# The 96 slots of an expert block laid on 128 partitions, three of each four, with ranks dealt round sixteen groups of partitions

## What is computed

```
xn2 = rmsnorm(x, ffn_norm_w)                    # (1088, 1024)
grp = argmax(xn2 @ w_rg + b_rg)                 # one of 4 groups
top_v, top_i = top_k(expert logits of that group (8), 2)
w   = softmax(top_v) * p_grp
expert_id = grp * 8 + top_i                     # 2 of 32 experts a token
for each block of tokens of one expert e:
    xb = xn2[idx]
    yb = (silu(xb @ w_gate[e]) * (xb @ w_up[e])) @ w_down[e]
y = x + sum over a token's two choices of w * yb
```

## Time and profile before

| | |
|---|---|
| time before, median of 3 runs | 1531.64 us (1528.09 to 1534.46) |
| the profiled execution, its own time | 1530.42 us |
| its span | 1528.7 us |
| mean granted TensorE clock | 0.977 |
| busy, share of the span: PE, DVE, ACT, POOL | 94%, 67%, 46%, 30% |
| weight queue (q1): moved, share of 16 DMA engines | 322.10 MB, 62.1% |
| row queue (q0): moved, share | 29.21 MB, 6.2% |

### The profile page before, as it was taken

One profiled execution on the slowest core, in us unless ns is written; L12 is line 12 of the kernel. 1 busy time (PEld: TensorE's weight loads), 2 busy tenths in 40 slices (PEclk: granted clock), 3 DMA queues, 4 the chain that ended last, 5 costly groups with the idle time before them and its releaser, 6 DMA issues.

```text
span 1528.7 us, 21704 instructions
## 1 busy us (share of the span) xinstructions
PE 1431.5 (94%) x8070; PEld 1207.7 (79%) x8070; DVE 1019.8 (67%) x1387; ACT 702.0 (46%) x830; POOL 458.9 (30%) x372
## 2 busy tenths in 40 slices
PE   7999999999999999999999789989999999999993
PEld 6899999989999998898887667767766666666662
DVE  4422321166677777777566889979988788888882
ACT  6321121154445544323121266757666666666670
POOL 1600000021111112001100475466755454555543
PEclk9999999999999999999999799999999999999996
DMA  5345449244333325676733799999999999999971
GB/s 195 117 154 167 160 160 104 97 148 137 106 101 101 101 76 149 186 241 212 314 119 124 249 355 375 382 362 365 363 357 353 348 351 346 349 360 354 369 276 32
DMA packets 156588, 352.34 MB, mean 230 GB/s; under 512 B 32098, under 2 KB 110374, under 8 KB 130849
## 3 DMA queue, kind: packets, MB, share of 16 engines
q1 hardware_dynamic: 134744, 322.10, 62.1%
q0 software_dynamic: 21248, 29.21, 6.2%
q10 hardware_dynamic: 536, 0.26, 0.1%
HBM read 308.80 MB, written 87.17 MB: 259 GB/s over the span
## 4 chain that ended last, share of the span: by engine, by line
DMA 24%; PE 19%; issue 4%; POOL 3%; DVE 2%; ACT 0%; POOLq 0%; ACTq 0%; SPq 0%; DVEq 0%
DMA w_out<-in_w_down_e 15%; DMA w_gate<-in_w_gate_e 2%; PE xt_ey L2794 1%; DVE e_w_lo L2648 1%; PE xt_ey L2796 1%; PE xt_ey L2795 1%; DMA y_rows<-group_rows,slot_table 1%; DMA first_rows<-y_rows 1%; POOL slot_info L2497 1%; DMA y_prompt<-y_rows,slot_table 1%; PE y_x L2202 1%; PE y_h_up L2202 1%; PE y_x L2204 1%; PE y_h_up L2204 1%; PE y_x L2203 1%
## 5 line engine op out<-in xcount | busy, mean ns | idle before, releaser
L2648 DVE TENSOR_TENSOR e_w_lo<-mixed,e_w_hi 128x2048 fp32r<-128x2048 f32 x64 | 145.2, 2286 | 11.5 <-ACT e_w_hi L2593 11.2
L2593 ACT CAST e_w_hi<-w_out 128x2048 fp32r<-128x2048 f32 x64 | 122.2, 1910 | 53.1 <-DMA w_out<-in_w_down_e 50.4
L2648 DVE TENSOR_TENSOR e_w_lo<-w_out,e_w_hi 128x2048 fp32r<-128x2048 f32 x64 | 143.8, 2284 | 2.2 <-ACT e_w_hi L2593 2.2
L2593 ACT CAST e_w_hi<-mixed 128x2048 fp32r<-128x2048 f32 x62 | 117.3, 1910 | 44.6 <-DMA mixed<-in_w_gate_e 30.9
L1018 PE MATMUL gate_banks<-f_hi,wg_hi 128*128 128x364 f32 (+1 forms) x376 | 126.8, 337 | 0.9 <-PEq L186 0.5
L2794 PE MATMUL xt_ey<-e_w_hi,e_hT_hi 128*96 128x512 f32 x256 | 105.0, 410 | 22.1 <-DVE e_w_lo L2648 22.1
L1019 PE MATMUL gate_banks<-f_lo,wg_hi 128*128 128x364 f32 (+1 forms) x376 | 123.5, 328 | 0.0
L1020 PE MATMUL gate_banks<-f_hi,wg_lo 128*128 128x364 f32 (+1 forms) x376 | 123.4, 328 | 0.0
L2796 PE MATMUL xt_ey<-e_w_hi,e_hT_lo 128*96 128x512 f32 x256 | 102.7, 401 | 0.0
L2795 PE MATMUL xt_ey<-e_w_lo,e_hT_hi 128*96 128x512 f32 x256 | 102.5, 400 | 0.0
L2772 PE MATMUL y_h_up<-e_w_hi,e_x_hi 128*96 128x512 f32 x256 | 100.7, 393 | 1.2 <-DVE e_w_lo L2648 1.1
(11 more groups left out here) (668 smaller groups left out, 3883.8 us busy)
## 6 DMA issues: line engine op xcount, KB each, us to landing
w_out<-in_w_down_e SPq DMA_DIRECT2D x64, 1024.0 KB, 30.6
mixed<-in_w_gate_e SPq DMA_DIRECT2D x32, 1024.0 KB, 30.6
mixed<-in_w_up_e SPq DMA_DIRECT2D x32, 1024.0 KB, 30.9
w_gate<-in_w_gate_e SPq DMA_DIRECT2D x32, 1024.0 KB, 31.3
w_up<-in_w_up_e SPq DMA_DIRECT2D x32, 1024.0 KB, 30.4
group_rows<-zeros SPq DMA_DIRECT2D x8, 1536.0 KB, 14.0
proj<-mixed SPq DMA_DIRECT2D x8, 1408.0 KB, 5.6
w_ring<-in_w_in SPq DMA_DIRECT2D x7, 1408.0 KB, 18.2
```

The lines of the kernel that those rows point to most:

```text
L2593: act.copy(hi(i, step, j), raw(i, u, j)).then_inc(hi_ready[i], 1)
L2648: dve.tensor_tensor(lo(i, u, j), raw(i, u, j), hi(i, step, j).bitcast(F32), ALU.subtract).then_inc(lo_ready[i], 1)
```

## The change

The block keeps 96 slots, but they are laid on all 128 partitions. Partition p holds a slot where p mod 4 is 0, 1 or 2; the fourth of each four holds none, ever. The rank r of the pair in partition p is given by writing p = 64a + 32b + 4c + d (a and b 0 or 1, c 0 to 7, d 0 to 2): r = 8a + 48b + c + 16d. So ranks 0 to 7 go to partitions 0, 4, ..., 28, ranks 8 to 15 to 64, 68, ..., 92, ranks 16 to 31 to the partitions one higher, and ranks from 48 on begin again at partition 32. In words: a group of partitions is four neighbours and the four that lie 32 higher, there are sixteen such groups, and consecutive ranks go to one group after the other. A block with 68 pairs has 4 or 5 of them in each group, where before its pairs were in partitions 0 to 67.

The row of numbers for the comparison is made in that order, with -1 (no rank) in each fourth place:

```diff
-        c.link(pool.iota(iota_i[:], pattern=[[1, P]], base=0, channel_multiplier=0))
-        c.link(pool.tensor_copy(row[:], iota_i[:, 0:SLOTS]))
+        c.link(pool.iota(iota_i[:], pattern=[[SLOTS // 12, 2], [SLOTS // 2, 2], [1, SLOTS // 12], [SLOTS // 6, LANES]], base=0, channel_multiplier=0))
+        c.link(pool.tensor_copy(row[:], iota_i[:]))
+        c.link(pool.memset(row[:].rearrange("p (q i) -> p q i", i=LANES)[:, :, KEPT:], -1.0))
...
-                ins = dve.tensor_tensor(s_hot[:, j * NR + t0:j * NR + t0 + nt], bc(by_choice(rank)[:, j, t0:t0 + nt], 2, SLOTS),
-                                        bc(row[:, 0:SLOTS], 1, nt), ALU.is_equal)
+                ins = dve.tensor_tensor(s_hot[:, j * NR + t0:j * NR + t0 + nt], bc(by_choice(rank)[:, j, t0:t0 + nt], 2, P),
+                                        bc(row[:], 1, nt), ALU.is_equal)
...
-                    ins = pe.matmul(Y[1][:SLOTS, o:o + NE], s_hot[:, j * NR + t, :], hot_tok[:, j, t, :],
+                    ins = pe.matmul(Y[1][:, o:o + NE], s_hot[:, j * NR + t, :], hot_tok[:, j, t, :],
```

`places` gets 13 more small instructions on DVE, which work out the partition from the rank:

```diff
+        for ap, n in ((by16, SLOTS // 6), (by8, SLOTS // 12)):
+            dve.tensor_scalar(ap, slot, 1.0 / n, 0.5 / n - 0.5, ALU.mult, ALU.add)
+        L(dve.tensor_scalar(by48, slot, 2.0 / SLOTS, 1.0 / SLOTS - 0.5, ALU.mult, ALU.add))
...
+        dve.tensor_tensor(by16, by16, by8, ALU.add)
+        L(dve.scalar_tensor_tensor(by48, slot, 4.0, by48, ALU.mult, ALU.add))
+        L(dve.tensor_tensor(slot, by16, by48, ALU.add))
+        dve.scalar_tensor_tensor(rel, rel, float(P), slot, ALU.mult, ALU.add)
```

The rows in SBUF, the tables of addresses and the scratch tensors get 128 rows for each block (`GROUP` is 1024 rows, not 768), and all row transfers are issued over 128 partitions:

```diff
-GROUP = EPG * SLOTS
+GROUP = EPG * P
...
-        R.xb = [nc.alloc_sbuf_tensor_at(f"x_rows{u}", [SLOTS, D], F32, offset=S["featT_at"] + 4 * D * u) for u in range(2)]
+        R.xb = [nc.alloc_sbuf_tensor_at(f"x_rows{u}", [P, D], F32, offset=S["featT_at"] + 4 * D * u) for u in range(2)]
...
-            pool.dma_start(group_rows[b][0:SLOTS, :], yb[b][:]).then_inc(rows_stored[b], 16)
-            pool.dma_start(first_rows[b * SLOTS:(b + 1) * SLOTS, :], yb[b][:]).then_inc(first_rows_stored[b], 16)
+            pool.dma_start(group_rows[b][0:P, :], yb[b][:]).then_inc(rows_stored[b], 16)
+            pool.dma_start(first_rows[b * P:(b + 1) * P, :], yb[b][:]).then_inc(first_rows_stored[b], 16)
```

On PE all transposes and products have 128 columns of weights where they had 96; the number of matmuls and of streamed columns stays:

```diff
-                o = 512 * (k // 4) + SLOTS * (k % 4)
-                ins = pe.transpose(X[:, o:o + SLOTS], xb[u][:, k:D:KD], S["ident"][:SLOTS, :SLOTS])
+                o = P * k
+                ins = pe.transpose(X[:, o:o + P], xb[u][:, k:D:KD], S["ident"][:])
...
-                pe.matmul(bank[:SLOTS, :], x_hi[u][:, k, :], w_hi[:, n, :], start=(k == 0), stop=False)
+                pe.matmul(bank[:], x_hi[u][:, k, :], w_hi[:, n, :], start=(k == 0), stop=False)
```

ACT and DVE still read and write 96 of a block's turned columns, now three of each four with a stride (`every` is true only for blocks 0 and 1, and for the first hidden rows, so that the fourth columns hold something once):

```diff
+    def lanes(ap, every):
+
+        return ap.rearrange("p (n i) -> p n i", i=LANES)[:, :, 0:LANES if every else KEPT]
...
-            act.copy(x_hi[u][:].rearrange("p (h k) t -> p h (k t)", h=2), x_psum).then_inc(s["x_hi_ready"], 1)
+            act.copy(x_split_of(x_hi[u][:], every), lanes(X[:, 0:C], every)).then_inc(s["x_hi_ready"], 1)
...
             if not first:
                 act.wait_ge(done[DOWN], 2 * b)
-            act.copy(h_hi[:].rearrange("p k t -> p (k t)"), HT[:, 0:KF * SLOTS]).then_inc(s["h_hi_ready"], 1)
+            else:
+                act.wait_ge(R.x2_stored, 16 * NR)
+                act.wait_ge(R.y_begun, 16 * NR)
+            act.copy(x_split_of(h_hi[:], first), lanes(HT[:, 0:KF * P], first)).then_inc(s["h_hi_ready"], 1)
```

More of the change, by code:

```diff
@@ L54 @@
 FE = 512
-SLOTS = 96
+SLOTS, LANES, KEPT = 96, 4, 3
 MAXB = NE + (2 * T) // SLOTS
@@ L146, in project @@
         dist = sb("dist", [P, 2 * P], I32)
-        zeros, nobody = sb("zeros", [SLOTS, D // 2]), sb("nobody", [SLOTS, INFO], U32)
+        zeros, nobody = sb("zeros", [P, D // 2]), sb("nobody", [P, INFO], U32)
         tile0 = S["first_proj_tile"]
@@ L260, in _ @@
                         for half in range(2):
-                            view = empty[n - 1].rearrange("(b s) d -> s b d", s=SLOTS)[:, :, half * D // 2:(half + 1) * D // 2]
+                            view = empty[n - 1].rearrange("(b s) d -> s b d", s=P)[:, :, half * D // 2:(half + 1) * D // 2]
                             sp.dma_start(view, bc(zeros[:], 1, view.shape[1])).then_inc(spare_filled, 16)
@@ L2300, in place @@
         return nc.alloc_sbuf_tensor_at("e_" + name, shape, dt, offset=S["featT_at"] + used - 4 * int(np.prod(shape[1:])))
-    xb, yb, used = R.xb, R.yb, 4 * 4 * D
-    x_hi, x_lo = ([place(f"x_{n}{u}", [P, KD, SLOTS], F32R) for u in range(2)] for n in ("hi", "lo"))
-    silu, h = place("silu", [SLOTS, FE]), place("h", [SLOTS, FE])
+    xb, yb, used = R.xb, R.yb, 2 * 4 * D
+    x_hi, x_lo = ([place(f"x_{n}{u}", [P, KD, P], F32R) for u in range(2)] for n in ("hi", "lo"))
+    silu, h = place("silu", [P, FE]), place("h", [P, FE])
     low = [[nc.alloc_sbuf_tensor_at(f"e_w_lo{u}{i}", [P, PIECE * 2], F32R, offset=R.w_at[u][i]) for i in range(3)] for u in range(2)]
@@ L2358, in expert_at, with x_split_of @@
         return EPG * (b % NG) + b // NG
-    x_psum = X[:, :].rearrange("p (h c) -> p h c", h=2)[:, :, 0:C // 2]
+    def lanes(ap, every):
+        return ap.rearrange("p (n i) -> p n i", i=LANES)[:, :, 0:LANES if every else KEPT]
+    def x_split_of(tile, every):
+        return lanes(tile.rearrange("p k t -> p (k t)"), every)
     def on_sync(sp):
@@ L2595, in x_split @@
         def x_split(b, u):
+            every = isinstance(b, int) and b < 2
             act.wait_ge(s["xT_full"], b + 1)
-            act.copy(x_hi[u][:].rearrange("p (h k) t -> p h (k t)", h=2), x_psum).then_inc(s["x_hi_ready"], 1)
+            act.copy(x_split_of(x_hi[u][:], every), lanes(X[:, 0:C], every)).then_inc(s["x_hi_ready"], 1)
         def h_split(b, first=False):
@@ L2608, in activate @@
                 act.wait_ge(s["h_ready"], b)
-            act.activation(silu[:], Gt[u][:SLOTS, :], ACT.Silu).then_inc(s["silu_ready"], 1)
+            act.activation(silu[:], Gt[u][:, :], ACT.Silu).then_inc(s["silu_ready"], 1)
         def step(b, u, tt, before, first=False, end=False):
@@ L2771, in hidden @@
                 k = KD // 2 * j + n
-                pe.matmul(bank[:SLOTS, :], x_hi[u][:, k, :], w_hi[:, n, :], start=(k == 0), stop=False)
-                pe.matmul(bank[:SLOTS, :], x_hi[u][:, k, :], w_lo[:, n, :], start=False, stop=False)
-                ins = pe.matmul(bank[:SLOTS, :], x_lo[u][:, k, :], w_hi[:, n, :], start=False, stop=(k == KD - 1))
+                pe.matmul(bank[:], x_hi[u][:, k, :], w_hi[:, n, :], start=(k == 0), stop=False)
+                pe.matmul(bank[:], x_hi[u][:, k, :], w_lo[:, n, :], start=False, stop=False)
+                ins = pe.matmul(bank[:], x_lo[u][:, k, :], w_hi[:, n, :], start=False, stop=(k == KD - 1))
             ins.then_inc(done[i], 1)
@@ L2827, in on_tensor @@
         for _ in range(5):
-            pe.matmul(Gt[0][:SLOTS, 0:4 * SLOTS], x_hi[1][:, 0, :], wide_x, start=True, stop=True)
+            pe.matmul(Gt[0][:, 0:4 * SLOTS], x_hi[1][:, 0, :], wide_x, start=True, stop=True)
         turn_hidden(2 * more + 1)
         for _ in range(5):
-            pe.matmul(Gt[0][:SLOTS, 0:4 * SLOTS], x_hi[1][:, 0, :], wide_x, start=True, stop=True)
+            pe.matmul(Gt[0][:, 0:4 * SLOTS], x_hi[1][:, 0, :], wide_x, start=True, stop=True)
         down(2 * more + 1, 1, 1)
@@ L2882 @@
 SCRATCH = [("proj", (T, CTOK)), ("gates", (NGT, P, T)), ("xh2", (T, D)), ("x2d", (T, D)),
-           *((f"group_rows{g}", (EPG * SLOTS, D)) for g in range(NG)), ("first_rows", (NG * SLOTS, D)), ("slot_info", (SLOTS * MAXB, INFO)), ("row_c", (H, T))]
+           *((f"group_rows{g}", (GROUP, D)) for g in range(NG)), ("first_rows", (NG * P, D)), ("slot_info", (P * MAXB, INFO)), ("row_c", (H, T))]
 class Routing:
@@ L2969, in build @@
         R.info_at = behind("info_at", [P, n], U32)[:]
-        R.table = behind("slot_table", [SLOTS, MAXB * INFO], U32)
-        R.fields = [behind(f"slot_fields{u}", [SLOTS, X_ROW - Y_ROW], U32) for u in range(2)]
-        R.first_at = behind("first_at", [SLOTS, 2 * NG], U32)
-        R.yb += [behind(f"y_rows{n}", [SLOTS, D]) for n in range(2, NG)]
+        R.table = behind("slot_table", [P, MAXB * INFO], U32)
+        R.fields = [behind(f"slot_fields{u}", [P, X_ROW - Y_ROW], U32) for u in range(2)]
+        R.first_at = behind("first_at", [P, 2 * NG], U32)
+        R.yb = [behind(f"y_rows{n}", [P, D]) for n in range(NG)]
+        R.hT = [behind(f"e_hT_{n}", [P, FE // P, P], F32R) for n in ("hi", "lo")]
         w_out_at = f_lo_at
```

64 lines of the change are left out of this document (36 added, 28 removed).

## The result

The changed kernel takes **1490.2 us** (median of 4, 1487.3 to 1491.7) beside 1533.1 us for the kernel before on the same chip: a ratio of 0.972, 95% interval 0.969 to 0.975. The forecast was 1495 us, range 1478 to 1520. The profiled execution of the change took 1491.7 us with a span of 1490.0; that of before had 1528.7, so the two traces differ by 38.7 us.

What follows compares the result with a forecast made beforehand. PE was taken to bound the experts until the weight queue's lead was used up, transfers from 1108 us on. From 1530.4 us profiled, -31 - 8 + 2.5 = -36.5 gave 1493.9, 1495 us as median; range 1478 to 1520.

Steps and rivals of the forecast that it cites:

- Item 1: Expert blocks from 1108 us on: gathered rows spread over all partition groups end slow transfers, 20.1 to 18.2 us a block, -31 us.
- item 6: No cost from POOL's memset, moved buffers, ACT's added waits; transfers naming 128 rows might show some 3 us at the end.
- Item 2: Matmuls on PE: 128 columns of weights instead of 96 cost 0, at most 0.2 us a block.
- item 5: The head: wider one_hots and x_split, 13 more places instructions, larger fills and stores cost +2.5 us, bounds 0 and +6.
- Item 3: Strided splits on DVE: at most +0.3 us a block, as much for hidden rows; hidden by PE, 0.
- Item 4: The end, after block 27's sum: rows land faster and the last two blocks shorten, -8 us, bounds 0 and -14.
- B: Rival: gathers themselves are slow; dealing only shortens slow stretches, 19.4 us a block, about 1520 us; chance 0.14.
- C: Rival: the mean transfer rate is a memory ceiling, so blocks still need 20.1 us, 1534 us; chance 0.08.
- D: Rival: rows touching all groups hurt all engines in the slow stretches, 20.9 us a block, 1547 us; chance 0.10.

Runs made afterwards that it cites:

- experiment 5: The changed kernel with 16 of a block's 72 matmuls left out (low half of the tokens in gate and up): 1477.0 us, ratio 0.964.
- experiment 4: The kernel of Experiment 1 with gathers and puts of rows naming only 112 partitions: 1546.1 us, ratio 1.007.
- Experiment 1: The changed kernel with the dealing taken back (rank r in partition r) and the 128-partition width kept: 1511.5 us, ratio 0.986.
- experiment 3: The kernel before, 96 wide, with its ranks dealt over its 96 partitions: 1514.4 us, ratio 0.988.
- experiment 8: The changed kernel with ranks in order on three of each four partitions and 16 of a block's 72 matmuls left out: 1493.6 us, ratio 0.974.

## Why the prediction was right, and where not

**Item 1, size.** Taken -31 us for 20.1 to 18.2 us a block; measured -34.5 for 20.2 to 18.1 over 16 blocks. The choice "a little above PE's floor" was too careful: PE is full. The transfers' 17.2 to 17.8 was 17.2 when measured by itself (experiment 5).

**Item 1, mechanism: this step failed.** That rows written into SBUF slow the weights beside them was right (experiment 4's two windows). But the prediction took the slow stretches as coming from rows "crowded in half of the partitions" and leaned on the stores of 64 rows at 186 GB/s. Experiment 1 has the rows in the same partitions and hardly a slow packet (2% over 355 ns, where it was 94%); experiment 4 has them there with 112-wide transfers, and the slow packets are back (97%). What slows the weights is that the gathers name fewer than 128 partitions, most likely because a share of rows then straddles two groups of partitions. Crowding has a cost of its own, but another and a smaller one, the load of the fullest group: 18.6, 17.9, 17.2 us a block for 8, 6, and 4 or 5 used partitions. The forecast was right since the change removes both. There was luck in it: that the transfers now name 128 partitions stands in the prediction as a possible cost (item 6), not as what would bring most of the gain. As it was put, item 1 would have given 20 us a block for experiment 1, 1.3 too much, and 18.1 to 18.6 for experiment 3, 1 too little. Its 64-row stores ran with nothing beside them: they show that such a transfer is itself slow, not that it slows the weights.

The rule that the prediction cited from the Trainium skill, SBUF — State Buffer, section "Door 1: The DMA port swizzle" (four neighbours and the four 32 higher share a port), fits what was measured if it is read with another rule of the Trainium skill: DMA: Bandwidth & Descriptors, section "The descriptor swizzle", says that in a transfer over 128 partitions each engine writes to one port. The 128-wide versions have hardly any slow packets (2% and 8% over 355 ns in the windows shown) and those with 96 and 112 have them (94% and 97%); that the shares follow these groups agrees with 17.2 and 17.9 us a block in experiments 5 and 8; that a straddling share writes to several ports was not observed, only the times that go with it.

**Item 2**: 0, measured 0 in the experts (0.93 against 0.92 us in 4 steps). But "wider weights cost nothing" was read from products of 512 columns and isn't true of the 28 products of 32 columns in `home_rows`, at a granted clock of 0.50: +1.5 us on PE, which item 5 lacked. **Item 3**: 0, measured 0; the bound of +0.3 was far off, a stride of 3 in 4 costs DVE nothing (950 against 952 ns). **Item 4**: -8, measured -8.1, with rows that land in 8.2, 6.3 and 3.6 us instead of 11.0, 7.4 and 6.5; but since experiment 1 gains nothing here, they land sooner for the dealing, not for quicker packets. **Item 5**: +2.5, measured +4.5, inside its bounds: 0.9 came before routing, 1.4 in it from `one_hots` and `home_rows` (the first low half starts at 866.9, not 864.6), 1.7 from PE's longer wait behind `places`, 0.5 is not assigned. **Item 6**: nothing found against it; POOL is busy 10.7 us a block (178.40 over 16.6 blocks), where it was 10.6.

**Rivals.** B described experiment 3, not the change. C, the mean as a ceiling: 415 GB/s over 292 us refute it. The Trainium skill, DMA: Bandwidth & Descriptors, section "Where 436 GB/s comes from", has a limit near 358 GB/s a core; the 415 lie above it, in a launch that runs on one core, and the measurement decides. D: spreading all rows over all groups hurt nothing, neither here nor in experiment 3 with its slow packets (1514.4 us, faster than before).

**What the profile was to show.** PE full, ACT's waits for `w_out` gone, matmul steps alike, the gather of `group_rows` in 8.2 us: all there. Windows behind gathers at 390 GB/s or more: not everywhere. One of the change moved 361 GB/s, with a median of 309 ns for its 285 weight packets (8% over 355) and 365 packets under 512 bytes:

```profile
DMA packets 784, 2.89 MB, mean 361 GB/s; under 512 B 365, under 2 KB 365, under 8 KB 499
...
q1 hardware_dynamic: 321, 2.33, 75.1%
q0 software_dynamic: 463, 0.55, 24.2%
```

There PE is the bound and pieces of weights land in 7.7 us, where they took 32 in the kernel before with its queue full, so a lower rate costs nothing; why it is 361 isn't settled.

## What to carry to other kernels

When small row transfers run beside a stream, lay them on all 128 partitions even if fewer hold data: here that alone, with the rows where they were, brought half of the gain, and 112 partitions were worse than 96. Then look at the fullest engine: rows and stream share it, and its packets times their duration gave the time of a block within 0.2 us in the 128-wide kernels. Compare a rate in windows with and without the suspected transfers before believing a mean, and test a layout by altering one property (width, order, share) at a time, since this change altered several.

## What the runs showed of the hardware that was not expected

- While gathers over 96 or 112 partitions bring rows of 4 KB into SBUF, the median 8 KB packet of another queue takes 401 to 426 ns; beside gathers over 128 partitions it is 309, at the same partitions in use. Plain stores of 96 rows out of SBUF leave them at 309, and so do, by the counts of rows, the indirect puts.
- 415 GB/s held for 292 us on one core with weights and rows mixed.
- A 128*128 product of 32 columns takes 221 ns where a 128*96 one takes 167, both at a granted clock of 0.50; of 512 columns both take 230 to 233, at 1.00. Short products at the full clock weren't compared.
- Left-out work on PE doesn't shorten a kernel whose transfers bound it, 1538 against 1535 us, though it left PE idle in 57 of 292 us.
